# Cached key and value pages handed over already turned, and loaded page by page through SyncE registers

## The chip, the cores and the metric

The kernel runs on one core of a Trainium2 chip. The metric is device time in microseconds (us) of one launch. The engines are PE (matrix products and transposes), DVE (vector), ACT (activations), POOL (GpSimd) and SP (SyncE, which only issues DMAs here); 16 DMA engines move data between HBM and SBUF (the on-chip memory).

## What is computed

One inference step of a two-layer decoder: a prompt of 256 tokens, and 8 decode streams of 4 new tokens each with 2048 cached positions. Layer 0 mixes tokens by an mLSTM, layer 1 by native sparse attention over a compressed, a selected and a window branch. After each layer a retrieval step (PEER) takes, for each token, 128 rows out of a table of 16,384 experts. The part that the change concerns reads the caches of layer 1:

```python
# cmp_kv, sel_kv: (pages, 128 tokens, K or V, 4 groups, 64); win_kv: (8 streams, 512, 2, 4, 64)
past_cmp = cache_cmp_kv[l, page_table]                       # 8 streams x 16 pages x 128 tokens
sub = kv.reshape(b, n // 16, 16, 2, 4, 64)                   # blocks of 16 tokens
first  = einsum('bnlcgd,cldh->bncgh', sub, w1[:, :16])
second = einsum('bnlcgd,cldh->bncgh', sub, w1[:, 16:])
ckv = einsum('bncgh,chd->bncgd', gelu(first[:, :-1] + second[:, 1:] + b1), w2)
o_cmp, p_cmp = attention(q, ckv)                             # compressed branch
o_sel = attention over the 16 blocks of 64 tokens that p_cmp selects, from past_sel
o_win = attention over the last 512 tokens, from win_kv
y = (g0 * o_cmp + g1 * o_sel + g2 * o_win) @ w_out
# PEER: out[n] = sum_k gate[n, k] * gelu(x[n] . u[e(n, k)]) * v[e(n, k)],  k = 0..127
```

## The kernel before

A short load stage brings tokens and constants in, and turns the page table into 128 x 32 row numbers (`quarter_idx`): a DMA on ACT's queue, a cast, a product with `page_rep`, five DVE instructions. The mLSTM layer follows, to about 375 us. The rest, up to a short final stage, is one long stage, `weave_stage`.

**The slots.** In `weave_stage` the PEER work of both layers runs as 576 slots. A slot is one indirect gather by POOL (L3076) of 128 rows of 8 KB (u and v of one expert per token, 1.05 MB) into a ring of nine buffers, a dot product on DVE (L3119), gelu, weight and a diagonal matrix on ACT (L3145, L3150, L3165), and two products on PE (L3193) or a fold on DVE (L3094). POOL runs ahead by up to the depth of the ring and waits for the last reader of a buffer.

**The beats.** All other work of layer 1, and the routing of both PEER layers, is woven between the slots in a fixed order. A slot has two beats (three in slots 20 to 56 and after 360); each engine's program is a generator that yields a beat number, and its instructions are put behind those of the slot to which the beat belongs. An engine takes its instructions in this order, so a wait of side work stops the slots behind it too. Side work comes in this order: the route of layer 0, `CachedBlocks`, the prompt's attention in two tiles (`PromptWork`), each with its routing (`RouteWork`), then `DecodeWork`.

**CachedBlocks** (compressed keys and values of the cached pages, beats 38 to 304). POOL gathers each stream's rows in four indirect DMAs (L1075, 128 rows of 8 KB, 16 tokens of one kind per 16 rows) into four buffers. PE turns them by `transpose` (L1090, 4 per step, 128 steps), ACT copies the turned blocks from PSUM to SBUF (L1139, 4 per step), and PE multiplies by w1 (L1101, one product per step). `split`, `meet`, `squash`, `outputs` and `store` make the branch's keys and values. SP loads w1 by four DMAs with rows of 256 bytes (L1057), w2 and the bias (L1059, L1061).

**PromptWork** compresses the prompt's own rows with the same weights, loaded again for each of two tiles (L1807, four DMAs of 256-byte rows); PE waits for them before L1450. The projection weights (L1342) of tile 0 may be loaded when the cached blocks' last turn is done.

**DecodeWork** has 20 parts (`PARTS`: 16 of the selected branch, four of the window), nine beats or three slots each. A part covers 512 positions of two streams: two tiles of 128 rows x 8 KB, loaded into a ring of six buffers by POOL (L2152, indirect, selected branch; POOL waits until the values of part p - 3 are summed) or by SP (L2594, window). PE turns the keys (`turn`, L2210, 16 transposes), ACT and DVE copy them (L2349, L2351, two each), PE multiplies the queries by them (`product`, L2220, four), then mask (L2477), maxima (L2492, one per part), exponentials (L2378), their transposes (L2240), a copy (L2367), and the products with the values (L2252).

Of the kernel before, what the change touches and what calls it, by code (L numbers as in the profile page):

```python
# [19 lines left out]
P = 128  # L20
# [24 lines left out]
def constants():  # L45
# [3 lines left out]
    def put(name, a):  # L49
# [46 lines left out]
    put("win_mask", [[[NEG if 4 * n_ + j < q[p] else 0 for n_ in range(P)] for j in range(4)] for p in i])  # L96
    put("pos16", np.repeat(i[:, None] % 8, DEC_B, 1))

    put("page_rep", [[float(r // 8 == p) for r in range(P)] for p in range(NPAGE)])
    put("stack32", [[float(p % NDEC == t) for t in range(NDEC)] for p in range(P)])  # L100
    head = ("tri", "tri_dec", "mask", "mask_dec", "sel_head", "last", "last_dec", "last_state", "seq_q", "seq_k",
            "page_rep", "pos16")
    order = list(head) + [name for name in cols if name not in head]
    n = 0
    for name in order:
# [6 lines left out]
HEAD = ("tri", "tri_dec", "mask", "mask_dec", "sel_head", "last", "last_dec", "last_state", "seq_q", "seq_k",  # L112
        "page_rep", "pos16")
# [828 lines left out]
class Shared:  # L942


    def __init__(self, nc, st, M, I, O, h, idx, gate, quarter_idx, added):
        self.nc, self.M, self.I, self.O, self.h, self.idx, self.gate = nc, M, I, O, h, idx, gate
        self.quarter_idx, self.added = quarter_idx, added
# [10 lines left out]
        self.w_in = [st.sem(f"w_in{i}") for i in range(2)]  # L958

# [65 lines left out]
class CachedBlocks:  # L1025


    START = 38
    UNIT = 2 * CSTR
    TILES = 4  # L1030

    def __init__(self, st, S, first, more):
        self.S, self.first = S, first
        place = S.slab.place
        self.rows = place(0, [P, self.TILES, ITEM])
        self.w1 = place(8192, [P, 2, CSTR // 2, 2, ADH])
        self.sub_T = place(10240, [P, 3, AG, P])
# [5 lines left out]
        self.bank = [S.bank[0], S.bank[3], *more]  # L1043
        self.ps_h = [S.bank[1 + c].rearrange("p (g n) -> p g n", g=AG) for c in range(2)]
        self.ps_k = S.bank[2][:, 0:2 * P].rearrange("p (a n) -> p a n", a=2)
        self.ps_v = S.bank[2][:, 2 * P:4 * P]
        (self.weights_in, self.turned, self.copied, self.multiplied, self.second_ready, self.pre_ready, self.hid_ready,
         self.out_mm, self.out_cp) = (st.sem(n) for n in (
             "cw_in", "c_turned", "c_copied", "c_multiplied", "c_second", "c_pre", "c_hid", "c_out_mm", "c_out_cp"))
        self.rows_in = [st.sem(f"c_rows_in{i}") for i in range(self.TILES)]  # L1050

    def load_weights(self, sp):
        I = self.S.I
        sp.wait_ge(self.first.projected, 2 * NJ)
        for c in range(2):
            for f in range(2):
                sp.dma_start(self.w1[:, c, :, f], I["nsa_cmp_w1"][0, c, f * CSTR:(f + 1) * CSTR].rearrange(  # L1057
                    "(k l) d h -> (l d) k h", l=2)).then_inc(self.weights_in, 16)
            sp.dma_start(self.w2[:, c], I["nsa_cmp_w2"][0, c]).then_inc(self.weights_in, 16)  # L1059
        with self.S.nc.allow_non_contiguous_dma(reason="128 biases"):  # L1060
            sp.dma_start(self.b1, I["nsa_cmp_b1"][0].rearrange("c h -> h c")).then_inc(self.weights_in, 16)  # L1061

    LOADS = 2 * 2 + 2 + 1

    def pool(self, pool, at):
        cache = self.S.I["cache_cmp_kv"][0].rearrange("a (n l) c g d -> (a n) (l c g d)", l=PTOK)
        for i in range(4 * DEC_B):
            b, e = divmod(i, 4)
            if i < self.TILES:
                yield from at(self.START - 20 + i // 2)  # L1070
                pool.wait_ge(self.first.projected, 2 * NJ)
            else:
                yield from at(self.START + 8 * (i - self.TILES) + 8)
                pool.wait_ge(self.turned, 4 * (i - self.TILES) + 4)
            pool.indirect_dma_start(self.rows[:, i % self.TILES, :], None, cache,  # L1075
                                    bass.IndirectOffsetOnAxis(ap=self.S.quarter_idx[:, e, b:b + 1], axis=0)
                                    ).then_inc(self.rows_in[i % self.TILES], 16)

    def turn(self, pe, q):
        i, c, k = q // 4, (q // 2) % 2, q % 2
        tile = self.rows[:, i % self.TILES, :].rearrange("p (k l c a gd) -> p k l c a gd", k=2, l=2, c=2, a=2)
        if q % 4 == 0:
            pe.wait_ge(self.rows_in[i % self.TILES], 16 * (i // self.TILES + 1))
        if q >= 4:
            pe.wait_ge(self.copied, q - 3)
        for l in range(2):
            for a in range(2):
                mm = pe.transpose(self.bank[q % 4][:, (2 * l + a) * P:(2 * l + a + 1) * P], tile[:, k, l, c, a, :],  # L1090
                                  self.S.M.ident)
        mm.then_inc(self.turned, 1)

    def product(self, pe, q):
        b, c, pair = q // CSTR, (q // 2) % 2, 2 * (q % CSTR // 4) + q % 2
        pe.wait_ge(self.copied, q + 1)
        if pair == 0 and b:
            pe.wait_ge(self.pre_ready, 2 * (b - 1) + c + 1)
            if c:
                pe.wait_ge(self.out_cp, 2 * b)  # L1100
        pe.matmul(self.ps_h[c], self.w1[:, c, pair].rearrange("p f h -> p (f h)"), self.sub_T[:, q % 3],  # L1101
                  start=(pair == 0), stop=(pair == CSTR // 2 - 1)).then_inc(self.multiplied, 1)

    def outputs(self, pe, b):
        pe.wait_ge(self.hid_ready, 2 * b + 2)
        for g in range(AG):
# [8 lines left out]
    def pe(self, pe, at):  # L1115
# [3 lines left out]
        for b in range(DEC_B + 1):  # L1119
            for r in range(0, self.UNIT if b < DEC_B else 8, 2):  # L1120
                yield from at(self.START + self.UNIT * b + r)
                q = CSTR * b + r // 2
                if b < DEC_B:
                    self.turn(pe, q)
                if 1 < q <= CSTR * DEC_B + 1:
                    self.product(pe, q - 2)
                if r == 6 and b:
                    self.outputs(pe, b - 1)
        self.S.leave(pe, self.out_cp, 2 * DEC_B)

    def copy(self, act, q):
        act.wait_ge(self.turned, q + 1)
        if q >= 3:
            act.wait_ge(self.multiplied, q - 2)
        tr = self.bank[q % 4].rearrange("p (l a n) -> p l a n", l=2, a=2)
        for l in range(2):
            for g2 in range(2):
                dst = self.sub_T[ADH * l:ADH * l + ADH, q % 3].rearrange("p (a g) n -> p a g n", g=2)[:, :, g2]
                ins = act.activation(dst, tr[ADH * g2:ADH * g2 + ADH, l], ACT.Copy)  # L1139
        ins.then_inc(self.copied, 1)  # L1140
# [17 lines left out]
    def act(self, act, at):  # L1158
# [3 lines left out]
        for b in range(DEC_B + 1):  # L1162
            for r in range(1, self.UNIT if b < DEC_B else 9, 2):
# [9 lines left out]
                if b == DEC_B:  # L1173
                    continue
# [2175 lines left out]
```

## Time and profile before

| | |
|---|---|
| time, median of 3 runs | 2576.49 us |
| lowest and highest | 2570.51 and 2578.44 us |
| the profiled execution, its time | 2571.7 us |
| its span | 2569.9 us |
| mean granted clock of PE, share of full speed | 0.861 |

The profile comes from one further execution, whose own time stands in the table beside its span; the span runs from its first to its last recorded instruction. Idle time of an engine is put down to the event that came last before it went on, its releaser. L numbers are lines of the kernel. `g_`, `f_` and the like ahead of a buffer's name are stages. PEld is PE's load of the stationary operand, which overlaps its products. A product of 512 columns in fp32 leaves two records. "PEq" and "SPq" are an engine's instruction queue, with its semaphore and DMA-issuing instructions.

### The profile page before, as it was taken

What the parts mean: (1) busy time and instruction counts of PE and PEld (TensorE: products, weight loads), DVE (VectorE), ACT (ScalarE), POOL (GpSimd) and SP (SyncE); (2) the same over time, 40 slices, a digit from 0 to 9 for tenths busy, and PEclk for the clock granted to TensorE, in tenths of its full rate; (3) what the DMA queues carried; (4) which work ended last, traced back from release to release, by engine and by line L of the source; (5) the groups of instructions that cost most, each with busy time, mean ns of one, the idle gap of its engine ahead of it and who ended that gap; (6) DMA issues with size and microseconds to landing.
All of it is one profiled execution on the core that took longest, in us unless ns stands there. A gap on an engine that the chain in (4) does not pass through costs nothing. (4 is left out here: it accounts for less than half of the span.)

```text
span 2569.9 us, 23064 instructions
## 1 busy us (share of the span) xinstructions
PE 1970.7 (77%) x6950; PEld 981.6 (38%) x6950; DVE 1468.7 (57%) x3134; ACT 916.4 (36%) x2462; POOL 942.9 (37%) x839
## 2 busy tenths in 40 slices
PE   5999797788888777977768688875677777739765
PEld 4436565344444334545212345362122333313211
DVE  1025256895666535774874455758447666664564
ACT  1112103687777323631232234412134444422222
POOL 2021033677554323342653332426233333122551
PEclk9975799899899888998889777987789899969979
DMA  6232518978999989898989986976789888989697
GB/s 194 99 143 74 172 54 334 367 320 345 420 420 420 413 332 388 348 405 302 411 347 387 351 328 229 368 292 270 309 339 358 346 346 347 353 291 359 244 420 296
DMA packets 170226, 805.61 MB, mean 313 GB/s; under 512 B 32564, under 2 KB 37176, under 8 KB 86648
## 3 DMA queue, kind: packets, MB, share of 16 engines
q0 software_dynamic: 93552, 673.78, 66.0%
q1 hardware_dynamic: 76408, 130.37, 14.2%
q8 instruction: 57, 0.93, 0.2%
q14 instruction: 65, 0.53, 0.1%
q10 hardware_dynamic: 144, 0.00, 0.0%
HBM read 798.37 MB, written 14.04 MB: 316 GB/s over the span
## 5 line engine op out<-in xcount | busy, mean ns | idle before, releaser
L3076 POOL DMA_INDIRECT g_uv<-in_peer_uv_dram,f_idx x320 | 389.6, 1217 | 642.0 <-PE g_acc L3193 512.3
L3193 PE MATMUL g_acc<-g_uv,g_diag 128*128 128x512 f32 (+1 forms) x848 | 451.7, 670 | 110.8 <-ACT g_diag L3165 109.1
L3119 DVE CUSTOM_DVE_ANT_0 g_uv<-g_uv,f_h 128x1024 f32<-128x1024 f32 x320 | 405.2, 1271 | 212.1 <-DMA g_uv<-in_peer_uv_dram,f_idx 204.4
L3076 POOL DMA_INDIRECT f_u<-in_peer_uv_dram,f_idx x256 | 299.6, 1170 | 491.9 <-PE g_acc L3193 383.9
L3119 DVE CUSTOM_DVE_ANT_0 f_u<-f_u,f_h 128x1024 f32<-128x1024 f32 x256 | 325.0, 1276 | 180.6 <-DMA f_u<-in_peer_uv_dram,f_idx 174.9
L3193 PE MATMUL g_acc<-f_u,g_diag 128*128 128x512 f32 (+1 forms) x676 | 356.4, 661 | 69.3 <-ACT g_diag L3165 51.7
L3145 ACT ACTIVATE g_gelu<-g_dot 128x2 f32<-128x2 f32 x288 | 58.3, 203 | 763.6 <-DVE g_dot L3119 762.4
L3193 PEld LDWEIGHTS g_acc<-g_uv,g_diag 128*128 128x128 f32 (+1 forms) x848 | 156.9, 197 | 353.3 <-issue 336.4
L3193 PEld LDWEIGHTS g_acc<-f_u,g_diag 128*128 128x128 f32 (+1 forms) x676 | 125.4, 198 | 254.8 <-issue 234.1
L1241 PE MATMUL g_side<-g_slab 128*128 128x512 f32 (+3 forms) x288 | 128.9, 589 | 55.0 <-DMA g_slab<-in_nsa_w_in_dram 52.4
L1101 PE MATMUL g_side<-g_slab 128*128 128x512 f32 x256 | 135.9, 613 | 13.6 <-ACT g_slab L1139 11.9
L3165 ACT ACTIVATE g_diag<-const,g_w 128x128 f32<-128x128 f32 (+1 forms) x381 | 135.8, 383 | 22.8 <-issue 0.7
L3094 DVE SCALAR_TENSOR_TENSOR x<-g_uv,g_w,x 128x1024 f32<-128x1024 f32 x108 | 138.4, 1281 | 7.6 <-ACT g_w L3150 7.6
L3150 ACT ACTIVATE g_w<-g_gelu,f_gate 128x1 f32<-128x1 f32 x576 | 138.2, 287 | 9.4
L3094 DVE SCALAR_TENSOR_TENSOR x<-f_u,g_w,x 128x1024 f32<-128x1024 f32 x87 | 112.3, 1291 | 1.2 <-ACT g_w L3150 1.2
L1139 ACT ACTIVATE g_slab<-g_side 64x256 f32<-64x256 f32 x256 | 96.9, 379 | 19.3 <-PE g_side L1090 15.7
L1939 POOL TENSOR_TENSOR g_slab<-g_slab 128x1024 f32<-128x1024 f32 (+1 forms) x20 | 49.1, 2453 | 144.6 <-DVE g_slab L1898 143.8
L2220 PE MATMUL g_side<-g_cmp_kT,g_q_blk 128*32 128x512 f32 x160 | 93.5, 671 | 10.7 <-DVE g_cmp_kT L2351 6.4
L1139 ACT ACTIVATE g_slab<-g_more 64x256 f32<-64x256 f32 x256 | 96.9, 379 | 9.4 <-PE g_more L1090 5.9
L1996 PE MATMUL g_side<-g_slab 128*128 128x128 f32 x512 | 67.6, 295 | 36.8 <-DMA g_slab<-in_peer_w_q_dram 36.8
L1241 PEld LDWEIGHTS g_side<-g_slab 128*128 128x128 f32 (+1 forms) x288 | 45.2, 176 | 130.6 <-issue 75.3
L290 PE MATMUL mp_acc<-mp_w,hc_h_T 128*128 128x512 f32 (+3 forms) x240 | 90.7, 531 | 0.0
(406 smaller groups left out, 2678.8 us busy)
## 6 DMA issues: line engine op xcount, KB each, us to landing
g_slab<-in_nsa_w_in_dram SPq DMA_DIRECT2D x15, 2048.0 KB, 19.1
g_slab<-in_peer_w_q_dram SPq DMA_DIRECT2D x14, 2048.0 KB, 22.2
mp_w<-in_mlstm_w_in_dram SPq DMA_DIRECT2D x6, 2048.0 KB, 10.0
g_slab<-in_nsa_w_out_dram SPq DMA_DIRECT2D x6, 2048.0 KB, 8.4
g_slab<-in_state_win_kv_dram SPq DMA_DIRECT2D x8, 1024.0 KB, 7.7
out_win_s_dram<-in_state_win_kv_dram SPq DMA_DIRECT2D x1, 8128.0 KB
g_uv<-in_peer_uv_dram,f_idx POOLq DMA_INDIRECT x320, 10.8
f_u<-in_mlstm_w_out_dram SPq DMA_DIRECT2D x2, 2048.0 KB, 11.0
```

The source lines that it names most:

```text
L290: mm = pe.matmul(acc[q % banks][0:nt, 0:n], M.h_T[:, c, t0:t0 + nt], w[:, j % WRING, c, 0:n], start=(c == 0), stop=(c == DC - 1))
L1101: pe.matmul(self.ps_h[c], self.w1[:, c, pair].rearrange("p f h -> p (f h)"), self.sub_T[:, q % 3], start=(pair == 0), stop=(pair == CSTR / ...
L1139: ins = act.activation(dst, tr[ADH * g2:ADH * g2 + ADH, l], ACT.Copy)
L1241: mm = pe.matmul(S.bank[2 + j % 2][0:n, 0:cols], self.h_T[s][:, c, 0:n], self.ring[s][:, j % 2, c, 0:cols], start=(c == 0), stop=(c == DC ...
L1996: mm = pe.matmul(S.bank[2 + j % 2][:, c * P:(c + 1) * P], self.proj.ring[0][:, j % 2, k, c * P:(c + 1) * P], self.proj.h_T[0][:, k, :], st ...
L2220: pe.matmul(self.bank[1][r0:r0 + 32].rearrange("p (l j) -> p l j", l=4), self.q_blk[:, 2 * PARTS[p][1] + b2, a, :], self.kt[:, e % 2], sta ...
L3076: pool.indirect_dma_start(both(i), None, table, bass.IndirectOffsetOnAxis(ap=idx[:, col:col + 1], axis=0), element_offset=layer * PK * PK ...
L3094: dve.scalar_tensor_tensor(out=M.x[:, t, :], in0=row(i, 1), scalar=w[:, i // GRP % WRING_UV, i % GRP:i % GRP + 1], in1=M.x[:, t, :], op0=A ...
L3119: dve.tensor_tensor_reduce(row(i, 0), row(i, 0), h[:, t, :], 1.0, 0.0, ALU.mult, ALU.add, dot[:, g % DRING, k:k + 1]).then_inc(dotted, 1)
L3150: ins = act.activation(w[:, g % WRING_UV, k:k + 1], gelu[:, g % 2, k:k + 1], ACT.Copy, scale=gate[:, col + k:col + k + 1])
L3165: act.activation(diag[:, q % DIAGS, 0:n], base, ACT.Copy, scale=w[:, i // GRP % WRING_UV, i % GRP:i % GRP + 1]).then_inc(diag_ready, 1)
L3193: mm = pe.matmul(acc[0:n, a, :], diag[:, q % DIAGS, 0:n], row(i, 1)[:, a * 512:a * 512 + 512], start=i == opens[s], stop=i == closes[s])
```

## The change

The host hands over the caches in another order. The compressed branch's pages come as `cmp_turned` (page, K or V, 128, 256), whose rows are already what the transposes made; the selected and the window caches as `sel_turned` and `win_turned`, rows of 2 KB and 8 KB with the keys turned and the values as before. w1 and w2 come as `cmp_w1_rows` (128 rows of 8 KB) and `cmp_w2_rows`.

The page table now stays as 128 integers on one partition of SBUF (`pages`). SP reads each page's number into a register with `value_load` and issues a direct DMA whose address holds that register. For `CachedBlocks` these are 16 units (stream, K or V) of 16 DMAs of 128 KB, with 128 rows of 1 KB each, into a ring of two units; 16 register loads per stream serve both units. The product reads the rows as they lie, its moving operand in runs of eight floats. For the selected parts there are eight DMAs of 256 KB each (128 rows of 2 KB), each with its own register load; the window's tiles come by direct DMAs as before. Removed are the transposes, the copies and POOL's gathers for the caches, the row numbers in the load stage and the constants for them. `CachedBlocks` starts at beat 32 where it started at 38, and ends at 299; a part's products wait for its tiles directly. The start of the projection weights' loads of tile 0 now waits for the last product of the cached blocks. In `DecodeWork` SP's program has the loads of all parts in order, with the saves of the finished outputs between them.

```diff
 class Shared:
+    def page(self, sp, b, k):
+        at = NPAGE * b + k
+        return sp.value_load(self.pages[0:1, at:at + 1], min_val=0, max_val=self.I["sel_turned"].shape[0] - 1)
 class CachedBlocks:
-    START = 38
-    UNIT = 2 * CSTR
-    TILES = 4
+    START = 32
+    UNIT = 16
+    UNITS = 2 * DEC_B
...
-    def load_weights(self, sp):
-        I = self.S.I
+    def sync(self, sp):
+        S, I = self.S, self.S.I
         sp.wait_ge(self.first.projected, 2 * NJ)
-        for c in range(2):
-            for f in range(2):
-                sp.dma_start(self.w1[:, c, :, f], I["nsa_cmp_w1"][0, c, f * CSTR:(f + 1) * CSTR].rearrange(
-                    "(k l) d h -> (l d) k h", l=2)).then_inc(self.weights_in, 16)
-            sp.dma_start(self.w2[:, c], I["nsa_cmp_w2"][0, c]).then_inc(self.weights_in, 16)
+        sp.dma_start(self.w1.rearrange("p c k f h -> p (c k f h)"), I["cmp_w1_rows"]).then_inc(self.weights_in, 16)
+        sp.dma_start(self.w2.rearrange("p c d -> p (c d)"), I["cmp_w2_rows"]).then_inc(self.weights_in, 16)
...
+        for b in range(DEC_B):
+            page = [S.page(sp, b, k) for k in range(NPAGE)]
+            for c in range(2):
+                v = 2 * b + c
+                if v >= 2:
+                    sp.wait_ge(self.multiplied, 8 * (v - 1))
+                for k in range(NPAGE):
+                    sp.dma_start(self.rows[:, v % 2, k, :], I["cmp_turned"][bass.ds(page[k], 1), c].rearrange(
+                        "u p n -> (u p) n")).then_inc(self.rows_in[v % 2], 16)
...
+    def product(self, pe, v, k):
+        b, c = divmod(v, 2)
+        if k == 0:
+            pe.wait_ge(self.rows_in[v % 2], 16 * NPAGE * (v // 2 + 1))
+            if v >= 2:
+                pe.wait_ge(self.pre_ready, v - 1)
+        rhs = self.rows[:, v % 2].rearrange("p a (k g n) -> p k g a n", k=8, g=AG)[:, k]
+        pe.matmul(self.ps_h[c].rearrange("p g (a n) -> p g a n", n=8), self.w1[:, c, k].rearrange("p f h -> p (f h)"), rhs,
+                  start=(k == 0), stop=(k == 7)).then_inc(self.multiplied, 1)
...
  class Projection:
-    def sync(self, sp, t, rows_turned=None):
+    def sync(self, sp, t, rows_used=None):
...
-                sp.wait_ge(rows_turned, CSTR * DEC_B)
+                sp.wait_ge(rows_used, CSTR * DEC_B)
  class PromptWork:
...
-        for c in range(2):
-            for f in range(2):
-                sp.dma_start(self.w1[:, c, :, f], I["nsa_cmp_w1"][0, c, f * CSTR:(f + 1) * CSTR].rearrange(
-                    "(k l) d h -> (l d) k h", l=2)).then_inc(self.cw_in, 16)
+        sp.dma_start(self.w1.rearrange("p c k f h -> p (c k f h)"), I["cmp_w1_rows"]).then_inc(self.cw_in, 16)
...
  class DecodeWork:
     def pool(self, pool, at):
...
-        yield from at(self.beat + 44)
-        pool.wait_ge(self.S.w_used, 24 + 6)
-        for p in range(3):
-            load(p)
-        for p in range(3, 16):
-            yield from at(self.PART0 + self.PB * (p - 3) + 18)
-            pool.wait_ge(self.summed, p - 2)
-            load(p)
...
      def sync(self, sp):
...
+        def load(p):
+            branch, u, q = PARTS[p]
+            if p >= 3:
+                sp.wait_ge(self.summed, p - 2)
+            for b2 in range(2):
+                slot = (2 * p + b2) % SLOTS
+                if branch:
+                    sp.dma_start(self.rows[:, slot, :], I["win_turned"][2 * u + b2]).then_inc(self.window_in[slot], 16)
+                    continue
+                for k in range(4):
+                    page = S.page(sp, 2 * u + b2, 4 * q + k)
+                    sp.dma_start(self.rows[:, slot, 2 * GD * k:2 * GD * (k + 1)], I["sel_turned"][bass.ds(page, 1)].rearrange(
+                        "u p n -> (u p) n")).then_inc(self.landed[slot], 16)
...
         sp.wait_ge(proj.saved, 16 * (6 + 2 + DEC_B))
+        sp.wait_ge(S.w_used, 24 + 6)
+        for p in range(3):
+            load(p)
         for u in range(4):
             sp.wait_ge(self.b_done, u + 1)
             save(0, u, self.o_cmp[:, u, :])
-        for u in range(3):
-            sp.wait_ge(self.o_ready, u + 1)
-            save(1, u, self.o[:, u, :])
-        for p in (16, 17, 18):
-            load_window(p)
+        for p in range(3, len(PARTS)):
+            load(p)
+            if p % 4 == 0 and p >= 8:
+                sp.wait_ge(self.o_ready, p // 4 - 1)
+                save(1, p // 4 - 2, self.o[:, p // 4 - 2, :])
...
  def load_stage(nc, M, I, pages):
...
+                sp.dma_start(pages[:], I["page_table"].rearrange("(u b) k -> u (b k)", u=1)).then_inc(loaded, 16)
```

## Rows read from the trace of the kernel before

**Rows 1.** The page's section 1, whole span: busy us, share, instructions.

```profile
PE 1970.7 (77%) x6950; PEld 981.6 (38%) x6950; DVE 1468.7 (57%) x3134; ACT 916.4 (36%) x2462; POOL 942.9 (37%) x839
```

**Rows 2.** The page's section 3, queues: packets, MB, share of 16 engines' time.

```profile
q0 software_dynamic: 93552, 673.78, 66.0%
q1 hardware_dynamic: 76408, 130.37, 14.2%
```

**Rows 3.** Windows: length, busy of PE, PEld, DVE, ACT, POOL, PEclk, DMA, GB/s.

```profile
511.00:540.00 29.00, 25.25 (x103) 13.51 (x102) 26.00 (x87) 26.51 (x71) 24.60 (x23) 1.00 0.68 263
420.00:639.00 219.00, 175.63 (x617) 90.25 (x615) 161.69 (x435) 150.42 (x408) 147.40 (x130) 0.91 0.88 347
639.00:835.00 196.00, 163.68 (x576) 83.55 (x576) 121.00 (x168) 144.03 (x408) 99.78 (x76) 0.93 1.01 420
978.00:992.00 14.00, 0.38 (x1) 0.00 (x0) 4.34 (x8) 2.95 (x12) 1.20 (x2) 0.71 1.02 412
1452.00:1469.00 17.00, 6.57 (x31) 6.60 (x32) 0.00 (x0) 0.00 (x0) 0.00 (x0) 0.50 0.82 309
1960.00:2200.00 240.00, 182.14 (x797) 74.94 (x795) 163.85 (x297) 99.83 (x202) 83.85 (x76) 0.92 0.88 345
```

**Rows 4.** Windows, the dots (L3119) alone, two instructions a slot.

```profile
639.00:835.00 196.00, 78.86 (x128) 0.93 1.01 420
1960.00:2200.00 240.00, 60.03 (x100) 0.92 0.88 345
```

**Rows 5.** Timeline of one line, the parts' maxima, one per part.

```profile
L2492 DVE TENSOR_REDUCE g_nmax<-g_slab x20: 686/687/722, 1972.7 to 2264.5; 128x1 f32<-128x512 f32 x12, 128x1 f32<-128x544 f32 x8
```

**Rows 6.** Timeline of the start, 0 to 16 us, all engines.

```profile
12.47 0.56 PE L3249 MATMUL ld_ps_rows<-ld_pages_f,hc_const 16*128 16x8 f32 x2 [12.47 <-DMA hc_const<-in_const_dram]
...
13.28 0.79 DVE L3237 TENSOR_SCALAR f_quarter_idx<-ld_row_f 128x8 uint32<-128x8 f32 x4
```

**Rows 7.** Groups of 420 to 855 us: busy, mean ns, idle before, releasers.

```profile
L1101 PE MATMUL g_side<-g_slab 128*128 128x512 f32 x256 | 135.9, 613 | 13.6 <-ACT g_slab L1139 11.9 <-ACT g_cmp_v L1156 1.5
L1139 ACT ACTIVATE g_slab<-g_side 64x256 f32<-64x256 f32 x256 | 96.9, 379 | 19.3 <-PE g_side L1090 15.7
...
L1090 PE MATMUL g_side<-const,g_slab 128*128 128x128 f32 x256 | 41.0, 285 | 12.5 <-issue 12.5
```

**Rows 8.** Timeline of SP's queue from 400 us: start, us, line, count.

```profile
420.13 0.99 SPq L1057 DMA_DIRECT2D g_slab<-in_nsa_cmp_w_dram  x2
...
427.40 19.84 SPq L1059 DMA_DIRECT2D g_slab<-in_nsa_cmp_w_dram  x1
```

**Rows 9.** DMA issues: times, KB each, median us to landing.

```profile
g_slab<-in_nsa_w_in_dram SPq DMA_DIRECT2D x15, 2048.0 KB, 19.1
g_slab<-in_peer_w_q_dram SPq DMA_DIRECT2D x14, 2048.0 KB, 22.2
...
g_slab<-in_state_win_kv_dram SPq DMA_DIRECT2D x8, 1024.0 KB, 7.7
...
g_slab<-in_nsa_cmp_w_dram SPq DMA_DIRECT2D x12, 256.0 KB, 18.4
...
ld_pages<-in_page_table_dram ACTq DMA_DIRECT2D x1, 0.5 KB, 5.3
```

**Rows 10.** Waits of the whole span: us in total, times, longest.

```profile
POOL g_slab L2152 <- PE g_side L2252: 71.0, 10, 10.5
...
PE g_side L1450 <- DMA g_slab<-in_nsa_cmp_w_dram: 30.5, 2, 16.8
```

**Rows 11.** Groups of 1960 to 2302 us, columns as in rows 7.

```profile
L2210 PE MATMUL g_side<-const,g_slab 128*128 128x128 f32 x160 | 29.3, 313 | 1.7 <-DVEq L2467 1.7
...
L2351 DVE COPY g_cmp_kT<-g_more 128x512 f32<-128x512 f32 x40 | 27.5, 688 | 68.5 <-PE g_more L2210 68.5
...
L2349 ACT ACTIVATE g_cmp_kT<-g_side 128x512 f32<-128x512 f32 x40 | 23.8, 594 | 95.2 <-PE g_side L2210 94.8
```

More of the change, by code:

```diff
@@ L1063 @@
[L1063 to L1077, printed above, removed]
@@ L1081, in turn @@
[L1081 to L1092, printed above, removed]
@@ L1094, in product @@
[L1094 to L1102, printed above, removed]
+        self.ps_k = S.bank[0][:, 0:2 * P].rearrange("p (a n) -> p a n", a=2)
@@ L1142, in split @@
-    def split(self, act, b, c):
-        act.wait_ge(self.multiplied, CSTR * b + (14, 16)[c])
-        if b:
-            act.wait_ge(self.pre_ready, 2 * (b - 1) + c + 1)
-        act.activation(self.second[:, c], self.ps_h[c][ADH:P], ACT.Copy).then_inc(self.second_ready, 1)
-    def squash(self, act, b, c):
-        act.wait_ge(self.pre_ready, 2 * b + c + 1)
-        act.activation(self.hid[:, c, :, 0:N_CMP], self.pre[:, c, :, 0:N_CMP], ACT.Gelu, bias=self.b1[:, c:c + 1]
-                       ).then_inc(self.hid_ready, 1)
+        for v in range(self.UNITS + 1):
+            for k in range(8):
+                yield from at(self.START + self.UNIT * v + 2 * k)
+                if v < self.UNITS:
+                    self.product(pe, v, k)
+                if k == 4 and v and v % 2 == 0:
+                    self.outputs(pe, v // 2 - 1)
+                    if v == self.UNITS:
+                        break
@@ L2145, in pool @@
     def pool(self, pool, at):
-        cached = self.I["cache_sel_kv"][0].rearrange("a (n l) c g d -> (a n) (l c g d)", l=PTOK)
-        def load(p):
-            _, u, q = PARTS[p]
-            for b2 in range(2):
-                slot = (2 * p + b2) % SLOTS
-                pool.indirect_dma_start(self.rows[:, slot, :], None, cached, bass.IndirectOffsetOnAxis(
-                    ap=self.S.quarter_idx[:, q, 2 * u + b2:2 * u + b2 + 1], axis=0)).then_inc(self.landed[slot], 16)
         yield from at(self.beat)
@@ L2195, in blocks_pe, with product @@
             mm.then_inc(self.b_summed, 1)
[L2197 to L2198 removed]
+    def product(self, pe, p, k):
+        b2, a = k // 2, k % 2
         slot = (2 * p + b2) % SLOTS
@@ L2356, in parts_act @@
             yield from at(beat)
-            p, r = divmod(beat - self.PART0, period)
-            if r in (1, 5) and p < n:
-                self.copy_keys(act, 4 * p + r // 2)
             q, r = divmod(beat - self.PART0 - 14, period)
@@ L2534, in parts_dve @@
             yield from at(beat)
-            p, r = divmod(beat - self.PART0, period)
-            if r in (3, 7) and p < n:
-                self.copy_keys(dve, 4 * p + r // 2)
             q, r = divmod(beat - self.PART0 - 9, period)
@@ L2942, in __init__ @@
         self.first = FirstRoute(st, S, self.ranks, self.route.keys_in, u_ring, v_ring, more, acc, w_out_in, d_scores)
-        self.cached = CachedBlocks(st, S, self.first, [more[:, 0], more[:, 1]])
+        self.cached = CachedBlocks(st, S, self.first)
         self.vec = st.sem("side_vec")
@@ L2949, in __init__ @@
             beat = self.beats[t][1] + self.route.length(t) + 8
-        assert self.beats[0][0] >= self.cached.START + DEC_B * self.cached.UNIT + 10
-        self.decode = DecodeWork(st, S, self.proj, self.ranks, max(beat, first_beat(DENSE)), q_blk, more[:, 0])
+        assert self.beats[0][0] >= self.cached.START + self.cached.UNITS * self.cached.UNIT + 11
+        self.decode = DecodeWork(st, S, self.proj, self.ranks, max(beat, first_beat(DENSE)), q_blk)
     def pool(self, pool, at):
-        yield from together(self.first.side_pool(pool, at), self.cached.pool(pool, at))
+        yield from self.first.side_pool(pool, at)
         for t, (_, second) in enumerate(self.beats):
```

240 lines of the change are left out of this document (88 added, 152 removed).

## Prediction

> **What bounds the kernel now.** I read the shares by engine first. PE leads with 1970.7 us, 77% of the span [rows 1], so neither engine nor queue is full everywhere, and the change has to be priced stage by stage. The second view is that of the queues: POOL's gathers (q0) hold 66.0% of the 16 DMA engines' time and SP's direct loads (q1) 14.2% [rows 2]. The third, the windows, shows where DMA is full: in 639 to 835 us, the second half of the cached blocks, its share is 1.01 at 420 GB/s; in 511 to 540 it falls to 0.68, over 420 to 639 it is 0.88, and over the decode parts 0.88 [rows 3]. So the stages that the change touches are held by DMA, fully or nearly.
>
> The pace follows from the dots (each slot has one dot and one accumulator read, so half the count is slots): 64 slots in 196 us are 3.06 us a slot, 50 slots in 240 us are 4.8 [rows 4]. The maxima, one per part, run from 1972.7 to 2264.5: 291.8/19 = 15.36 us a part [rows 5]. A part holds three slots (3 x 1.05 MB) and two tiles (2 x 1.05 MB), 5.24 MB; at 420 GB/s that is 12.5 us, so some 2.9 us of each part are not transfer. The reader is to see two things: work taken from PE, ACT and DVE is worth nothing where DMA is at 1.01, and is worth something in the parts, if it is what keeps DMA from running.
>
> **Price of a packet.** Queue rows give means: q0 0.66 x 2569.9 us x 16 / 93552 = 290 ns for 7.2 KB, q1 76 ns for 1.7 KB [rows 2]. A straight line through both is an estimate of 10 ns a packet and 0.039 ns a byte: 1 KB 50 ns, 2 KB 90 ns, 256 B 20 ns. For 8 KB I take 312 ns, from 420 GB/s over 16 engines [rows 3] (the line says 328). A slot or tile is 128 rows over 16 engines, eight such packets on each.
>
> **Load stage.** Gone is the chain after the constants: the matmul starts at 12.47, the last index is made at 13.28 + 0.79 = 14.07, while the constants alone would end it at 12.5 [rows 6]. SP issues one small DMA more (0.4 us). Term: -1 us.
>
> **Cached blocks.** Removed: 512 transposes (41.0 us busy for the 256 of one bank, the other's are like them) and 512 ACT copies of 379 ns (194 us) [rows 7], and 32 POOL gathers. The 128 products stay, at 613 ns a record [rows 7]; their moving operand is now read in runs of 8 floats. No row shows such a read; the bounds are nothing and a doubling (+136 us of PE), and as some 80 us of transposes leave the stage, half of them in the stretch where PE is busy 164 of 196 us [rows 3], I take nothing; with +136 (half of it there) that stretch would hold 164 - 40 + 68 = 192 of 196 us, so PE would just become its bound. Added: 256 page DMAs of 128 rows of 1 KB and 128 register loads on SP. The bytes stay 32 x 1.05 MB; the engine time goes from 256 packets x 312 = 80 us to 2048 x 50 = 102, +22 us per engine. w1's load goes from 256-B rows (256 packets x 20 = 5 us) to 8-KB rows (8 x 312 = 2.5). About half of the stage's 415 us is full, so +20 x 196/415 = +10 us land on the path. Against that: the weights' four 256-KB loads kept SP blocked 19.84 us [rows 8] and PE's first turn waiting 12.5 us [rows 7]; a megabyte of 8-KB rows lands in 7.7 us [rows 9]; then the pages of unit 0 are late next, so -6, not -12. And the 26 idle DMA us of 420 to 639 (0.12 x 219) arise while POOL is busy with other work and issues neither gathers nor cached rows; SP's loads no longer wait for POOL, of which I count -6. Term: -2 us, bounds -25 and +35.
>
> Two issues of 256 KB went out within 0.99 us, and such loads land in 18.4 us [rows 8, 9]: issues don't wait for landings, so 16 pages take 16 x 0.5 = 8 us of SP, beside the 26 us in which the eight slots of a unit's 16 beats and its 2 MB pass (64 x 0.312 + 128 x 0.05). The Trainium skill ("DMA: Bandwidth & Descriptors", Anatomy of one DMA) fits a DMA with a fixed 2.0 us plus its bytes over 436 GB/s; were pages in series, 16 x 2.3 = 37 us a unit would be an estimate from it, against those 26. The trace's two issues in 0.99 us speak against series.
>
> **A wait moved.** Prompt 0's projection weights now wait for the last product (beat 286) where they waited for the last turn (292): nothing, with 10 beats left before their use.
>
> **Prompt compression.** PE waits for w1 twice, 30.5 us together, 16.8 the longest [rows 10]; w1 comes there too as 256-B rows. As one load of 8 packets per engine it lands in some 5 to 8 us [rows 9], behind SP's earlier loads as before, so both waits go. In the first (978 to 992) DMA was at 1.02 meanwhile [rows 3]: gathers filled the ring, so half of the 13.7 comes back later as waits for gathers: -6. In the second (1452 to 1469) DMA was at 0.82 with POOL idle [rows 3], so the stall was lost time: -14. Term: -20, bounds -10 and -30.
>
> **Decode parts.** Removed per part: 16 transposes (29.3 us busy over 20 parts for one of two banks, so some 2.9 us a part for both), two ACT copies of 594 ns and two DVE copies of 688 ns, which sat idle 94.8 and 68.5 us for turns [rows 11]; two POOL gathers, before which POOL stood 71.0 us for the values of an older part [rows 10]. Behind that wait on POOL stand the next slots' gathers: that is what keeps DMA at 0.88. After it, SP waits instead, and behind SP stand only later loads and small saves. Added: 8 register loads and 8 DMAs of 256 KB per part. Transfer per part: 24 packets x 312 + 64 x 90 ns = 13.2 us against 12.5. The period can thus fall from 15.36 to 13.2 at best; I take 13.85, for one wait in three stays (the chain exp, turn, values keeps its order): -1.5 x 20 = -30. Bounds 0 and -43.
>
> **Register load.** No row shows one. Bounds: nothing, and 5.3 us, the landing of the 0.5-KB page DMA [rows 9]. It moves four bytes and no rows, so it is nearest to SP's own issue, 0.99/2 us [rows 8]: 0.5. That gives 8 x (0.5 + 0.5) = 8 us a part beside 13.85, and 16 x 0.5 + 32 x 0.5 = 24 us per pair of units beside 52. Hidden in both; the cover is gone at 13.85/8 - 0.5 = 1.2 us a load in the parts.
>
> The Trainium skill (the same page, Latency and other measured facts) gives `tensor_load` a floor of about 600 ns: an estimate of 8 x 1.1 = 8.8 us a part, hidden too. No run here shows it.
>
> **Sum** against the profiled 2571.7: -1 - 2 - 20 - 30 = -53, 2519. The median of the runs is 4.8 above the profiled time, their lowest 1.2 below it; I say 2520.
>
> **Rivals.** (1) SP becomes the bound: if a register load takes 2 us, a part takes 8 x 2.5 = 20 us: 16 x 4.64 = +74 there, -6 in the four window parts, -23 elsewhere, 2617. It equals the time before where 16 x (8 x (load + 0.5) - 15.36) = 29, at 1.65 us a load, and is slower from there. For it: no row prices the load. Against: it would have to cost more than three issues. 0.09.
> (2) Page packets starve. Loads of 2 MB in 2-KB rows (64 packets per engine) land in 19.1 and 22.2 us [rows 9], 300 to 347 ns a packet: about one 8-KB packet goes by with each small one. At 1 KB a unit needs 128 x 0.36 = 46 us while gathers keep coming, and has 26. The ring of nine slots then fills, gathers stop, and pages run alone; what is lost is what PE and DVE can't catch up. If that is 4 us a unit, +64: 2583. It ends slower from 53/16 = 3.3 us a unit on. For it: DMA is full at 639 to 835. Against: while pages are late, DMA isn't idle. 0.11.
> (3) Most is hidden: the parts stay at 14.9 (PE's clock and chain), the prompt gives 10: -1 - 2 - 10 - 9, 2550. 0.20.
> (4) Everything gives: parts at 13.2, all 30 us, gaps filled: -1 - 15 - 30 - 43, 2483. 0.15.
> The forecast has 0.45.
>
> **Numbers.** Faster by over 0.3% (7.7 us, about what a measurement of this kernel can tell from no change): forecast, (3), (4): 0.80. Of (1) and (2), 0.07 lie near their break-even, 0.13 are slower. Range 2475 to 2585: it takes in (3), (4) and the mild end of (2).
>
> **What would show it.** Right: no wait for w1 before L1450's work; maxima 13.5 to 14.2 us apart; POOL without waits for the values; the full stretch of the cached blocks at about 3.2 us a slot; SP's page issues about 1 us apart. Wrong: page issues over 1.9 us apart in the parts, PE waiting for cached rows with DMA below 0.9, products longer than 613 ns, or an unchanged part period with PE or the chain exp, turn, values as its releaser.

## The result and the profile after

The changed kernel takes 2546.72 us (median of 7 runs, 2531.91 to 2555.26) against 2576.49 before (7 runs, 2561.61 to 2581.72); the ratio is 0.9898, 95% interval 0.9875 to 0.9921. That is 26 to 30 us less, where 56 had been forecast. The profiled execution took 2555.3 us, the longest of its runs; its span is 16.5 us shorter than that of the profiled execution of before, and only these 16.5 us can be put to places below. The experiments left eleven more profiles, and where they differ from this one the text says so.

The page of the changed kernel, its engines and then its two main queues, for [rows 1] and [rows 2]:

```profile
PE 1883.3 (74%) x6116; PEld 896.6 (35%) x6116; DVE 1441.5 (56%) x3088; ACT 701.7 (27%) x1910; POOL 862.1 (34%) x775
...
q0 software_dynamic: 84336, 606.67, 59.8%
q1 hardware_dynamic: 119418, 197.43, 21.6%
```

PE lost 87 us of work, q1 took 43,010 more packets and 67 MB more; q0 gave up the same bytes in 9,216 packets.

Where the 16.5 us came from is read from the dots (one per slot), whose starts stand in the trace. This table is worked out from them (start in us; the last column is after minus before):

```
slot   before    after   difference   what lies ahead of it
   0    380.9    379.7      -1.1      load stage, mLSTM
  16    446.3    435.1     -11.2      first loads of the cached blocks
  32    511.3    510.2      -1.2      cached blocks, first units
  64    639.0    632.6      -6.4      cached blocks, dense part
 128    835.3    856.5     +21.1      cached blocks, full part
 144    886.8    907.6     +20.8      projection of tile 0
 368   1677.8   1691.2     +13.4      both prompt tiles
 432   1976.3   1975.7      -0.6      decode, up to the parts
 496   2302.4   2286.8     -15.6      decode parts
 575   2549.1   2532.9     -16.2      rest
```

So, from one mark to the next, the cached blocks cost 22 us, the prompt gave 7, the stretch ahead of the parts 14, the parts 15.

Windows of the changed kernel (length, busy of PE, PEld, DVE, ACT, POOL, PEclk, DMA share, GB/s): the full part of the cached blocks, which answers to 639 to 835 in [rows 3]; four pieces of one pair of units in it; and the decode parts.

```profile
632.00:856.00 224.00, 133.79 (x329) 59.26 (x330) 121.20 (x168) 47.92 (x153) 73.07 (x66) 0.80 0.95 369
690.00:720.00 30.00, 11.91 (x36) 5.25 (x34) 18.82 (x26) 7.39 (x24) 7.29 (x7) 0.72 1.02 413
720.00:729.00 9.00, 3.70 (x5) 1.64 (x6) 3.67 (x5) 1.09 (x4) 0.00 (x0) 0.50 1.01 332
729.00:732.00 3.00, 3.00 (x7) 1.25 (x6) 0.00 (x0) 0.00 (x0) 0.94 (x1) 0.72 0.04 13
732.00:744.00 12.00, 12.00 (x30) 5.30 (x29) 4.77 (x6) 1.68 (x5) 7.54 (x7) 1.00 0.95 358
1960.00:2200.00 240.00, 162.62 (x558) 48.56 (x555) 154.92 (x284) 88.76 (x183) 67.97 (x55) 0.85 0.96 374
```

The first row holds 64 slots in 224 us, 3.50 a slot, against 3.06 [rows 4]; DMA is at 0.95 and 369 GB/s where it was at 1.01 and 420. The next four show why. From 690 to 720 gathers and pages run together at full rate. From 720 to 729 POOL issues nothing and 1-KB rows run alone: share 1.01, but 332 GB/s, that is 1024 B/(332/16 GB/s) = 49 ns a packet, the estimate's 50. From 729 to 732 the DMA engines stand (0.04). From 732 gathers run alone. The end of POOL's wait, then PE's timeline over the same stretch:

```profile
731.06 0.94 POOL L2988 DMA_INDIRECT f_u<-in_peer_uv_dram,f_idx  x1 [23.87 <-PE g_acc L3105]
```

```profile
703.70 1.02 PE L1075 MATMUL g_side<-g_slab 128*128 128x512 f32 x2
725.30 2.08 PE L1075 MATMUL g_side<-g_slab 128*128 128x512 f32 x2 [20.57 <-DMA g_slab<-in_cmp_turned_dram]
727.17 3.62 PE L3105 MATMUL g_acc<-f_u,g_diag 128*128 128x512 f32 x4
```

PE stood 20.57 us before the first product of a unit, for rows that were not in. Their first DMA had been issued at 684.8: 128 rows an engine in 40 us, 0.32 us a row, while 690 to 720 was full of 8-KB gathers; about one of these went by with each (the trace's records of 690 to 720 hold 1342 rows of 8 KB and 1331 of 1 KB). The Trainium skill ("DMA: Bandwidth & Descriptors", Queues, rings and completion order) has the engines take turns between queues by packets of several descriptors; the trace agrees that turns are taken by count and not by bytes, and doesn't tell single rows from bunches of eight. SP's issues of these pages (min/median/max ns) feel it too:

```profile
L1065 SPq DMA_DIRECT2D g_slab<-in_cmp_turned_dram x256: 332/333/4622, 430.9 to 818.4; - x128
```

Of the 16 issues that began at 684.8, the first ten went out 0.51 us apart, and each of the last six held SP for 2.3 to 4.3 us; eight of the 16 units look like this. 2.3 us for the eight rows of one DMA on each engine are 0.29 us a row, so SP, too, gets on at the pace of about one 8-KB row for each small one. Over the span PE's waits for rows are these, beside the mask's wait for the parts' last product (us in total, times, longest):

```profile
PE g_side L1075 <- DMA g_slab<-in_cmp_turned_dram: 141.6, 9, 22.7
...
DVE g_slab L2384 <- PE g_side L2142: 74.0, 15, 12.2
```

The product itself is no slower for its runs of eight floats: the median of its records (min/median/max ns) is 592 ns, and 595 in the kernel before, whose line is the first; the longest ran at the low clock. (The means are 640 and 613 [rows 7], since more of them now fall to the low clock.)

```profile
L1101 PE MATMUL g_side<-g_slab x256: 592/595/1193, 473.0 to 839.0; 128*128 128x512 f32 x128
...
L1075 PE MATMUL g_side<-g_slab x256: 592/592/1222, 456.1 to 851.8; 128*128 128x512 f32 x128
```

The loads now (times, KB, median landing), and what SP spends on a register (min/median/max ns):

```profile
g_slab<-in_cmp_turned_dram SPq DMA_DIRECT2D x256, 128.0 KB, 7.2
g_slab<-in_sel_turned_dram SPq DMA_DIRECT2D x128, 256.0 KB, 7.2
...
g_slab<-in_cmp_w_rows_dram SPq DMA_DIRECT2D x3, 1024.0 KB, 7.1
```

```profile
L958 SPq TENSOR_LOAD <-f_pages x256: 260/268/732, 421.4 to 2167.3; - x128
L958 SPq FUSED_REGOPS  x256: 147/152/189, 422.2 to 2167.6; - x128
```

w1 lands in 7.1 us where its quarters took 18.4 [rows 9]; no wait of PE for it is left [rows 10]. A register costs SP 268 + 152 ns and an assertion of its bounds of 18, and 0.55 us lie between one register and the next. The parts' maxima, for [rows 5]:

```profile
L2399 DVE TENSOR_REDUCE g_nmax<-g_slab x20: 686/686/721, 1972.6 to 2249.9; 128x1 f32<-128x512 f32 x12, 128x1 f32<-128x544 f32 x8
```

277.3/19 = 14.59 us a part; 15.36 before, 13.85 forecast.

### The profile page after: what moved, and what is told of

Read it like the earlier page. It is cut to its first block and busy times, and to the rows that moved or that the text cites. A ratio compares the mean times of both kernels' runs of the same rounds, so it can differ in the third digit from the quotient of the medians.

```text
span 2553.4 us, 22375 instructions
## 1 busy us (share of the span) xinstructions
PE 1883.3 (74%) x6116; PEld 896.6 (35%) x6116; DVE 1441.5 (56%) x3088; ACT 701.7 (27%) x1910; POOL 862.1 (34%) x775
## 5 line engine op out<-in xcount | busy, mean ns | idle before, releaser
L2988 POOL DMA_INDIRECT g_uv<-in_peer_uv_dram,f_idx x320 | 380.8, 1190 | 733.7 <-PE g_acc L3105 598.5
L3031 DVE CUSTOM_DVE_ANT_0 f_u<-f_u,f_h 128x1024 f32<-128x1024 f32 x256 | 318.5, 1251 | 209.0 <-DMA f_u<-in_peer_uv_dram,f_idx 203.1
L1075 PE MATMUL g_side<-g_slab 128*128 128x512 f32 x256 | 134.0, 640 | 141.6 <-DMA g_slab<-in_cmp_turned_dram 141.6
L1075 PEld LDWEIGHTS g_side<-g_slab 128*128 128x128 f32 x256 | 51.5, 206 | 210.0 <-DMA g_slab<-in_cmp_turned_dram 126.5
L2142 PE MATMUL g_side<-g_slab,g_q_blk 128*32 128x512 f32 x160 | 97.6, 710 | 20.7 <-DMA g_slab<-in_sel_turned_dram 8.7
```

Source lines behind the costliest of these rows:

```text
L1075: pe.matmul(self.ps_h[c].rearrange("p g (a n) -> p g a n", n=8), self.w1[:, c, k].rearrange("p f h -> p (f h)"), rhs, start=(k == 0), stop ...
L2142: pe.matmul(self.bank[1][r0:r0 + 32].rearrange("p (l j) -> p l j", l=4), self.q_blk[:, 2 * PARTS[p][1] + b2, a, :], self.tiles[:, slot, :, ...
L2988: pool.indirect_dma_start(both(i), None, table, bass.IndirectOffsetOnAxis(ap=idx[:, col:col + 1], axis=0), element_offset=layer * PK * PK ...
L3031: dve.tensor_tensor_reduce(row(i, 0), row(i, 0), h[:, t, :], 1.0, 0.0, ALU.mult, ALU.add, dot[:, g % DRING, k:k + 1]).then_inc(dotted, 1)
```

## The experiments

All are edits of the changed kernel ("after" below, 2547 us, ratio 0.9898), each with its own ratio to the kernel before, taken on the same chip. The edits are shown shortened; "..." marks what is left out.

### Cached pages as rows of 2 KB

```diff
-self.rows = place(0, [P, 2, NPAGE, GD])
+self.rows = place(0, [P, 2, NPAGE // 2, 2 * GD])          # K and V of 8 pages
...
-for c in range(2): ... for k in range(NPAGE): dma(rows[:, v % 2, k], cmp_turned[page[k], c])
+for half in range(2): ... for k in range(NPAGE // 2): dma(rows[:, u % 2, k], cmp_turned[page[k]])
...
-product(v, k): 512 columns, one per step
+product(u, c, k): 256 columns (8 pages), two per step
```

> The changed kernel with one difference: a cached page comes as one DMA of 128 rows of 2 KB (keys and values side by side) where it came as two of 128 rows of 1 KB; the ring of two units holds half a stream each, and a product covers 256 columns where it covered 512. Bytes, page registers and slots stay. Theory A (small packets: each 1-KB packet lets an 8-KB packet of the gathers by, so that a unit's pages come late, PE stands, the ring fills and DMA pauses): half as many packets, so a unit's 64 packets find the 64 of its eight slots; the waits of 16 to 23 us for cached rows go, 16 slots of the full stretch take 52 to 53 us instead of 55 to 57, and the time falls by 15 to 22 us against the changed kernel, to about 2527. Rival B (SP: 128 register loads of 0.55 us): the same number of registers, so no more than 3 us change. Rival C (products with runs of eight floats bound PE): twice as many products, so the time rises.

2525.18 us, ratio 0.9802 [0.9776, 0.9828], 22 us below after. Slots 64 to 128, as a window of this kernel, and the wait for cached rows in it (85.0 us, 5 times, at most 22.7 in the same slots of after):

```profile
626.00:826.00 200.00, 136.87 (x438) 84.00 (x438) 121.89 (x168) 47.02 (x153) 76.45 (x65) 0.85 1.02 414
```

```profile
PE g_side L1075 <- DMA g_slab<-in_cmp_turned_dram: 47.3, 7, 7.5
```

200 us for 64 slots, 3.12 a slot, DMA at 1.02. The registers were the same 128 for the cached blocks, the products twice as many, of half the columns: theory A had the size right, and B and C fall. A rival that no expectation names falls as well: after's ring holds two units of 2 MB where the kernel before had four tiles of 1 MB, and this run keeps the two units.

### Cached blocks of before, the rest as changed

```diff
-CachedBlocks with page DMAs on SP
+CachedBlocks of before: indirect gathers on POOL, turns, copies (START 38); load stage makes quarter_idx
+self.w1 and self.w2 from cmp_w1_rows, cmp_w2_rows, one DMA each
```

> The changed kernel with the cached blocks of before (POOL gathers of 8-KB rows, transposes, ACT copies, starting at beat 38, and the row numbers in the load stage), but with w1 and w2 loaded as 8-KB and 512-B rows; the decode parts and the prompt stay as changed. Theory A: the cached stage costs the changed kernel about 22 us, which come back, with some 5 us more for the weights' loads: about 2520. Rival B (the cached stage is as fast as before, and the gain in the decode parts is what is small): within 5 us of the changed kernel.

2519.42 us, ratio 0.9795 [0.9768, 0.9821]. Slots 64 to 128 of this kernel:

```profile
628.00:822.00 194.00, 165.35 (x576) 86.30 (x576) 120.90 (x168) 143.99 (x408) 99.24 (x76) 0.91 1.01 423
```

194 us, as before the change. PE has 165 us of work there instead of 134 and ACT 144 instead of 48, and the stretch is 30 us shorter: what was taken from PE and ACT here was worth nothing, as forecast, and the pages cost 28 to 30 us against the gathers that they replaced. Its dots are at -13.7 us of before at slot 144 and -1.4 at slot 0, so the 8-KB weights alone gave some 12 us there. (In this kernel the page table lies on eight partitions instead of one; SP reads it for the selected pages alone.)

### No register loads

```diff
-return sp.value_load(self.pages[0:1, at:at + 1], ...)
+return at
```

> The changed kernel without its 256 register loads: every page DMA, of the cached blocks and of the decode parts, has a constant address (page numbers 0 to 127 in order instead of the page table's), so the outputs of the decode streams are those of other pages. Theory A (packets): no change, within 4 us. Rival B (register loads, 0.55 us each, hold SP up for 9 us a stream in the cached blocks and 4.4 us a part): the cached stage loses its waits for rows and the time falls by 10 us or more.

2554.10 us, ratio 0.9926 [0.9903, 0.9949]: no gain. It is 7 us above after where theory A allowed 4, with intervals that overlap. Its dots are at +22.1 us at slot 144, as after's +20.8. Taking away SP's registers and their 0.44 us brings nothing; the rival falls.

### w1 as 256-byte rows again

```diff
-sp.dma_start(self.w1..., I["cmp_w1_rows"])
+for c, f in 2 x 2: sp.dma_start(self.w1[:, c, :, f], I["nsa_cmp_w1"][...])      # in all three places
```

> The changed kernel with w1 loaded by four DMAs of 256-B rows, as before the change, in the cached blocks and in both prompt tiles. The 8-KB rows are what took the two waits before L1450 away: expected are waits of about 14 and 17 us there again and a time 14 to 20 us above the changed kernel's; rival: the waits stay away because SP gets to these loads earlier, and the time stays within 5 us.

2575.39 us, ratio 0.9999 [0.9979, 1.0019]: the whole gain of the change is gone, more than expected. In the profile, which is 21 us above after's, 8 of them arise in the cached blocks (+28.6 at slot 144; PE's first wait for rows is 32.5 us, and 22.3 in after) and 6 in the prompt (15, if the prompt's gain here, 1.6 us, is set against the 16.6 that is the middle of ten other profiles, see below); the last 7, in the decode, aren't explained. One of the two waits came back:

```profile
PE g_side L1409 <- DMA g_slab<-in_nsa_cmp_w_dram: 15.2, 1, 15.2
```

The first did not; no row tells why.

### Cached pages as rows of 512 bytes

```diff
-rows[:, v % 2, k, :]                    <- cmp_turned[page, c]  (128 rows of 1 KB)
+rows[:, v % 2, k].rearrange(h=2)        <- cmp_turned[page, c]  (2 x 128 rows of 512 B)
```

> The changed kernel with the cached pages' rows cut in two: each page DMA moves the same 128 KB as 256 rows of 512 B where it moved 128 of 1 KB; the number of DMAs, registers and products stays. Theory A in its two halves: if the price is the packets' own time (about 28 ns for 512 B against 49 ns for 1 KB, so 256 x 28 - 128 x 49 = 0.9 us a unit), the time rises by about 15 us; if it is that each small packet waits for a gather's packet, the rows come no later than before once the ring is full, since the gathers can send no more than the slots take, and again only the packets' own time and a longer stand of PE are added: 10 to 20 us above the changed kernel, 2557 to 2567, with waits for cached rows longer than 20 us at each unit. Rival (rows land late because of their number alone, every packet at one gather packet's time): 128 packets more a unit at 0.31 us, 40 us a unit, over 600 us more in all.

2571.44 us, ratio 0.9979 [0.9958, 1.0000], 21 to 25 us above after: a little past the upper end. PE waits 150.0 us for cached rows, 8 times, at most 25.0, against after's 141.6, 9 times: longer, but not over 20 us at every unit, as had been expected. The rival's 600 us are out. With 2 KB, 1 KB and 512 B the time is 2525, 2547 and 2571.

### Parts 3 to 15 without their loads

```diff
 def load(p):
     if p >= 3: sp.wait_ge(self.summed, p - 2)
+    if 3 <= p < 16: return
```

> The changed kernel without the loads of the selected parts 3 to 15: they compute on the six tiles of parts 0 to 2, and 26 x 1.05 MB with their DMAs and registers are left out (the outputs of the decode streams are not those of their own rows). Theory D (the parts are bound by DMA, which fell short of the forecast because the 2-KB rows fill it): 2 MB less of 5.24 MB a part, so the period falls from 14.6 us to the pace of the slots on the other engines, 12 us or less, and the time by 30 us or more. Rival E (the chain product, mask, maxima, exponentials, transposes, values, with the slots between, sets the period): the period stays above 14 us and the time falls by less than 10 us.

2547.64 us, ratio 0.9884 [0.9851, 0.9916]: no change. The maxima, the parts' window and the mask's wait:

```profile
L2401 DVE TENSOR_REDUCE g_nmax<-g_slab x20: 685/686/721, 1964.0 to 2238.6; 128x1 f32<-128x512 f32 x12, 128x1 f32<-128x544 f32 x8
```

```profile
1960.00:2200.00 240.00, 162.21 (x573) 48.70 (x572) 155.10 (x278) 89.38 (x182) 65.17 (x52) 0.86 0.70 266
```

```profile
DVE g_slab L2386 <- PE g_side L2144: 70.8, 15, 9.4
```

14.45 us a part with 2 MB less to move and DMA at 0.70. Transfers don't bound the parts of the changed kernel, and theory D falls; that it is the order, as rival E says, the next two runs bear out.

### Products ahead of the transposes

```diff
-if r in (2, 4, 6, 8): self.product(pe, p, r // 2 - 1)
+if r in (2, 3):
+    self.product(pe, p, 2 * r - 4)
+    self.product(pe, p, 2 * r - 3)
```

> The changed kernel with a part's four products on beats 2, 2, 3, 3 of its nine, ahead of the transposes of the exponentials of the part before, where they stood on beats 2, 4, 6, 8; the loads and everything else stay. Theory E (order: with the turns gone the products still stand where the turns' pace had put them, one beat ahead of the mask, so DVE waits 74 us for the last product and the slots' dots wait behind it): the mask's wait falls below 20 us, the period from 14.6 to 13.0 to 13.8 us, the time by 15 to 30 us. Rival (the tiles then come too late, since they are wanted five beats earlier): PE waits for them instead, and the period stays above 14.3.

2534.77 us, ratio 0.9862 [0.9826, 0.9898], some 10 us below after, with intervals that overlap a little; the expectation was 15 to 30. The maxima, then the waits that were 74.0 us for the mask and 8.7 for tiles:

```profile
L2400 DVE TENSOR_REDUCE g_nmax<-g_slab x20: 686/686/720, 1961.3 to 2232.0; 128x1 f32<-128x512 f32 x12, 128x1 f32<-128x544 f32 x8
```

```profile
PE g_side L2142 <- DMA g_slab<-in_sel_turned_dram: 56.1, 13, 11.4
...
DVE g_slab L2385 <- PE g_side L2142: 24.6, 4, 14.7
```

14.25 us a part, where 13.0 to 13.8 had been expected. The mask's wait fell to 24.6 us, not below 20, and a wait for tiles of 56.1 us took its place: both the theory and its rival were half right.

### The same, without the loads

Both edits at once.

> The changed kernel with the products on beats 2, 2, 3, 3 and without the loads of the selected parts 3 to 15 (those parts compute on the tiles of parts 0 to 2). Theory: two limits lie close behind each other in the parts, first the order of the work, then the tiles' transfers; without both the period falls to 13 us or less (from 14.25 with the early products alone and 14.45 without the loads alone), the waits of 56 us for tiles go, and the time is 15 us or more below that of the early products alone, about 2520 or less. Rival (the early products took away all that can be had): the period stays above 13.9 and the time within 8 us of 2535.

2497.83 us, ratio 0.9731 [0.9697, 0.9766], 34 to 37 us below the early products alone.

```profile
L2402 DVE TENSOR_REDUCE g_nmax<-g_slab x20: 686/686/720, 1966.8 to 2193.7; 128x1 f32<-128x512 f32 x12, 128x1 f32<-128x544 f32 x8
```

226.9/19 = 11.94 us a part. Two limits lie behind each other: with both the period is 14.59, with either one left 14.25 to 14.45, with neither 11.94. The edit takes out the tiles' bytes together with the waits for them, so it doesn't tell whether the second limit is DMA's time or the lateness of the tiles.

### Versions that put both together

> The kernel with the cached blocks of before and the rest as changed, with the products on beats 2, 2, 3, 3 as well. If both causes add up, 2519 less the gain of the early products: 2490 to 2505. If the parts were bound by transfers, 2519.

2503.82 us, ratio 0.9757 [0.9720, 0.9794], as expected if both add up.

> The kernel with cached pages as 2-KB rows, with the products on beats 2, 2, 3, 3 as well. If both causes add up, 2525 less the gain of the early products: 2495 to 2510; else 2525.

2515.49 us, ratio 0.9791 [0.9755, 0.9827], above what was expected: by the ratios only 3 us below the 2-KB rows alone. Its six runs spread from 2500.88 to 2526.96. In the profiles the early products made the parts 7 to 13 us shorter in each of the three pairs (with 1-KB rows, with 2-KB rows, with the old gathers), but no single pair of times shows it clear of noise.

> The kernel with the cached blocks of before and the rest as changed, with the products on beats 3, 3, 4, 4, still ahead of the transposes of the exponentials on beat 4: the tiles are wanted two beats later than with 2, 2, 3, 3, and the mask still stands four beats behind. If the waits for tiles are what is left, 3 to 8 us below 2504; if the later products meet the mask or the transposes, 2504 or above.

2500.80 us, ratio 0.9737 [0.9712, 0.9763]. It is 3 us below the first one, whose interval it overlaps, so the two beats can't be told apart. The two are the fastest kernels here that compute the whole step: cached blocks as before the change, weights in 8-KB rows, turned pages only in the decode, and the products moved.

## Why the prediction was wrong, step by step

**The cached blocks are the step that failed.** The term was -2 us; it measured +22, inside its stated bounds of -25 and +35, and the five profiles with 1-KB pages and w1 in 8-KB rows have 20 to 25. The packets' own price was right (49 ns alone; by the packet records of the runs 30 ns for 512 B, 86 for 2 KB, 315 for 8 KB). Wrong was the sentence that set rival (2) aside, "while pages are late, DMA isn't idle". It is idle when the rows have come: the ring is full, POOL waits for PE, PE takes up its products, and no transfer is asked for until it frees a slot (729 to 732). The rival's mechanism was there, at 24/16 = 1.5 us a unit more than forecast instead of its 4. In slots 64 to 128 the 28 us are worked out thus: DMA's idle share, 0.05 x 224 = 11 us where there was none before; 49 ns for each 1-KB row where an eighth of an 8-KB packet is 39, eight units x 128 x 10 ns = 10 us, which the forecast had; 4 us for the gathers' own packets, 323 ns on average there and 315 before; the last 3 aren't separated. The experiment with 2-KB rows takes back 24 of the 28 us, that with the old gathers all of them. The sentence "issues don't wait for landings" failed with it: it rested on two issues, and here it held for the first ten of a unit.

**The early lead was no gain.** Dots led by 11.2 us at slot 16, and by 1.2 at slot 32. Before, POOL asked for the first four tiles of cached rows from 423.6 us on, ahead of gathers of these slots; four tiles of 1.05 MB at 420 GB/s are 10 us. Now the first page is asked for at 430.9, behind the weights on SP's queue, and PE's first product waits longer than the 12.5 us of the first turn [rows 7]. The first loads of before, and the first wait of after:

```profile
L1075 POOL DMA_INDIRECT g_slab<-in_cache_cmp_kv_dram,f_quarter_idx x32: 936/941/3752, 423.6 to 792.1; - x32
```

```profile
PE g_side L1075 <- DMA g_slab<-in_cmp_turned_dram: 22.3, 1, 22.3
```

So the same rows were moved later. All nine profiles with pages have this lead, 9 to 10 us between slots 0 and 16, with w1 in 256-byte rows too, and the three with the old gathers don't have it. The -6 for the weights stood: they are worth some 8 us in the cached blocks with pages (20.8 against 28.6) and 12 with the old gathers. With the same weights the pages thus cost the stage 22 + 12 = 34 us against the gathers, where the sum had +10 and -6.

**The idle of 420 to 639** was to shrink by 6. It did shrink, to a DMA share of 0.95 from 0.88, but mostly with dearer packets (356 GB/s beside 347), and PE waited for rows: slots 16 to 64 took 197.5 us against 192.7.

**Prompt: -20 forecast, -7 in this profile.** Both waits went, as forecast. Slots 160 to 176 gained 7.5 us and 176 to 192 gave back 7.8; the second stall gained 12.6 at slot 308 and had 7.3 left at 340. But this profile is a low one: in the ten others whose prompt has w1 in 8-KB rows, slots 144 to 368 are 4 to 21 us faster than before, in six of them by 16 or more. So the term isn't shown to be wrong. Of the first stall, with DMA full, 0 to 5 of 7 to 10 us stayed in these ten, at most about half.

**Decode: -30 forecast, -29 measured, by luck.** The parts gave 15, at 14.59 us instead of 13.85. "One wait in three stays" named the wrong wait: it was the mask behind the last product, 74.0 us, since the products kept the beats that the turns had set. In the kernel before, the same wait was 15.0 us:

```profile
DVE g_slab L2477 <- PE g_side L2220: 15.0, 7, 2.7
```

Half the gain fell ahead of the parts (14 us, 11 of them between slots 408 and 412, and 10 to 11 there in every profile of the experiments), which no term held. There POOL used to issue six tiles of 1 MB in a row before the next slots' gathers; the first and the last of the six, the next gather, and SP's loads in after:

```profile
1886.29 0.94 POOL L2152 DMA_INDIRECT g_slab<-in_cache_sel_kv_dram,f_quarter_idx  x1 [0.30 <-issue]
...
1894.58 1.15 POOL L2152 DMA_INDIRECT g_slab<-in_cache_sel_kv_dram,f_quarter_idx  x1 [0.30 <-issue]
1896.03 0.93 POOL L3076 DMA_INDIRECT g_uv<-in_peer_uv_dram,f_idx  x1 [0.30 <-issue]
```

```profile
1894.26 46.33 SPq L2504 DMA_DIRECT2D g_slab<-in_sel_turned_dram  x24
```

SP's tiles now go by beside the gathers. That this is the cause is read from the order of the issues alone; no run tested it.

**The load stage** gave 1.1 for 1. **The register** costs 0.44 us for 0.5, and rival (1) had no part: the run without registers is no faster, and in the parts SP's issues are 1.1 us apart, as forecast. The Trainium skill ("DMA: Bandwidth & Descriptors", Latency and other measured facts) puts the floor of a `tensor_load` at about 600 ns; its record here is 268 ns long.

**The sum.** By the profiles -1 + 22 - 7 - 14 - 15 = -15, beside 16.5. The medians differ by 30, so some 13 us of the gain fell in executions that weren't profiled. With the middle of the ten prompts, 16.6 in place of 7, the sum would be -25, near the 26 to 30 of the times; that the prompt is the place is likely, and not shown.

## What to carry to other kernels

When transfers move from one queue to another, compare the size of their packets with those that they run beside: small ones take turns with large ones, come late, and cost engine time, which no count of bytes shows. Where DMA is full, a stall removed is mostly time borrowed: here 0 to 5 of 7 to 10 us stayed. A lead at one mark is no gain yet either: look whether the transfers ahead of it were only moved behind it. And when work is taken out of a fixed order, move up what stood behind it, or the old pace stays: here the products kept the turns' beats.

## What the runs showed of the hardware

Rows of 1 KB run alone at 332 GB/s, 8-KB gathers beside them at 413 together. PE stood until 725.3; in 720 to 729 its granted clock was 0.50, the lower of its two levels, 1.2 GHz, and 1.00 again in 732 to 744 after it had been working. With less work on PE, and its waits for rows, its mean clock in the full stretch fell from 0.93 to 0.80 (0.85 with 2-KB rows), and in the parts from 0.92 to 0.85, where the mean of the same product grew from 671 to 710 ns. A register read from SBUF and checked takes SP 0.44 us, about as much as the issue of a DMA behind it (0.51 us from one to the next); in units that ran beside gathers the last six of 16 issues mostly took 2.3 us or more each.
